# Four blocks of a modulation product moved from the full head pairs into the last head pair of an attention stage

## The reference

```
mod_l = split(silu(c)     @ ada_w[i] + ada_b[i], 6)     # for i = 0, 1
mod_c = split(silu(c_ctx) @ ada_w[i] + ada_b[i], 6)
q, k, v = h @ w_qkv + b_qkv                             # layer 0
o = softmax(q k^T * 64**-0.5 + bias) v                  # window keys + all context keys
x = x + gate * (o @ w_o + b_o)
```

## Time and profile before

| | |
|---|---|
| median of 3 executions | 2804.71 us |
| the profiled execution | 2803.35 us |
| its span (first to last instruction) | 2801.6 us |
| TensorE busy | 2571.0 us, 92% of the span |
| VectorE, ScalarE, GpSimd busy | 1082.8, 865.5, 478.1 us |
| line 687 (the ada blocks), TensorE | 384 matmul records, 49.6 us of record time |
| line 720 and 725 (pieces), TensorE | 296.2 and 151.6 us |
| line 570 (`rows`), VectorE | 20 instructions, 13.7 us |
| mean granted TensorE clock | 0.962 of full |

### The profile page before, as it was taken

How to read it: one execution, slowest core, us unless ns; L and a number is a source line. 1 busy time by engine, 2 the same in 40 slices (tenths; PEclk the granted TensorE clock), 3 DMA queues, 4 the chain that set the end, 5 groups by cost and what they waited for, 6 DMA issues and landing times. The chain is left out here.

```text
span 2801.6 us, 68712 instructions
## 1 busy us (share of the span) xinstructions
PE 2571.0 (92%) x28274; PEld 1803.8 (64%) x28275; DVE 1082.8 (39%) x2462; ACT 865.5 (31%) x1881; POOL 478.1 (17%) x590
## 2 busy tenths in 40 slices
PE   7999999999989849999999599999998699999990
PEld 6888788878745537777777484455444477777770
DVE  3134333433454532222222366556665322222225
ACT  3222322323210003333333355334500133333333
POOL 0111111121121012222222210000020122222223
PEclk9999999999999969999999799999999799999995
DMA  6322223132345287999999740000232999999995
GB/s 260 120 97 100 95 104 134 61 126 74 140 152 200 75 355 305 416 416 395 416 416 416 268 144 30 31 30 30 115 150 105 389 403 416 417 416 416 416 368 183
DMA packets 128670, 644.72 MB, mean 230 GB/s; under 512 B 18865, under 2 KB 31441, under 8 KB 72609
## 3 DMA queue, kind: packets, MB, share of 16 engines
q1 hardware_dynamic: 94912, 540.05, 48.5%
q0 software_dynamic: 17984, 57.16, 5.7%
q10 hardware_dynamic: 15648, 45.71, 4.2%
HBM read 578.29 MB, written 64.57 MB: 229 GB/s over the span
## 5 line engine op out<-in xcount | busy, mean ns | idle before, releaser
L1668 PE MATMUL PS<-wt,xT 128*32 128x256 f32 x13056 | 752.9, 381 | 38.3 <-DVE xT L1797 25.3
L1668 PEld LDWEIGHTS PS<-wt,xT 128*32 128x32 f32 x13056 | 513.0, 111 | 238.7 <-issue 47.9
L1613 ACT ACTIVATE y<-PS 32x256 f32<-32x256 f32 x816 | 306.3, 375 | 304.2 <-PE PS L1683 297.0
L1683 PE MATMUL PS<-wt,hidT 128*32 128x256 f32 x6528 | 395.2, 379 | 3.5 <-ACT y L1613 3.5
L1797 DVE STREAM_TRANSPOSE xT<-xg 128x256 f32<-128x256 f32 x206 | 91.8, 446 | 664.2 <-PE PS L1668 655.0
L1683 PEld LDWEIGHTS PS<-wt,hidT 128*32 128x32 f32 x6528 | 256.8, 110 | 99.3 <-issue 4.4
L720 PE MATMUL PS<-hT,slab 128*128 128x256 f32 x1280 | 296.2, 386 | 6.3 <-DVE low L613 3.5
L720 PEld LDWEIGHTS PS<-hT,slab 128*128 128x128 f32 x1280 | 239.9, 192 | 42.9 <-issue 6.5
L433 POOL TENSOR_SCALAR prob<-prob,inv 128x640 f32<-128x640 f32 (+2 forms) x80 | 130.3, 1629 | 662.2 <-DVE inv L628 662.2
L1573 POOL DMA_INDIRECT xg<-h_d,ib x212 | 208.3, 983 | 166.8 <-POOL ib L1570 166.0
L511 ACT ACTIVATE prob<-prob,low 128x640 f32<-128x640 f32 (+2 forms) x160 | 117.6, 735 | 300.2 <-DVE low L613 300.2
(11 more groups left out here) (247 smaller groups left out, 2653.4 us busy)
## 6 DMA issues: line engine op xcount, KB each, us to landing
wt<-in_w SPq DMA_DIRECT2D x256, 1024.0 KB, 11.9
wt<-in_w2s SPq DMA_DIRECT2D x128, 1024.0 KB
aw<-in_ada_w SPq DMA_DIRECT2D x48, 1024.0 KB, 4.9
ys_d<-y ACTq DMA_DIRECT2D x204, 128.0 KB
slab<-in_slabs SPq DMA_DIRECT2D x24, 512.0 KB, 3.3
tab<-in_tables SPq DMA_DIRECT2D x8, 1408.0 KB, 7.5
ys_d<-zero POOLq DMA_DIRECT2D x4, 2560.0 KB, 9.6
x_d<-x_p ACTq DMA_DIRECT2D x18, 512.0 KB, 4.8
```

What stands on the lines that cost most here:

```text
L1613: ins = a.activation(y[rows, q * QD:q * QD + QD], PS[STRIP * q:STRIP * q + STRIP, DOWN, 0:QD], ACT.Copy)
L1668: mm = t.matmul(PS[32 * g:32 * g + 32, UP, 0:QD], xT[:, k * 32:k * 32 + 32], wt[b][:, q, c * 1024 + g * QD:c * 1024 + g * QD + QD], start= ...
L1683: mm = t.matmul(PS[32 * g:32 * g + 32, DOWN, 0:QD], hT_[:, k * 32:k * 32 + 32], wt[b][:, q, c * 1024 + g * QD:c * 1024 + g * QD + QD], sta ...
```

## The change

The counts by pair change, and the last pair gets a list of how many blocks each of its ten units takes. Pairs 2, 3, 5 and 6 do one block fewer each, units 70, 71, 72 and 74 do two (the second one after values(i-1)), units 73, 75, 76 and 77 one. All 48 blocks are still done in the same order, and the last one still in unit 77.

```diff
-        BLOCKS = (5, 5, 5, 5, 4, 4, 4)
+        BLOCKS, LATE = (5, 5, 4, 4, 4, 3, 3), (2, 2, 2, 1, 2, 1, 1, 1, 0, 0)
...
             else:
-                if t < KD:
-                    first.append(("ada", KD + sum(BLOCKS) + t))
+                n = KD + sum(BLOCKS) + sum(LATE[:t])
+                if LATE[t]:
+                    first.append(("ada", n))
+                if LATE[t] > 1:
+                    second.append(("ada", n + 1))
             return first, second
```

## The result

The changed kernel takes 2809.18 us (median of 20 runs) beside 2804.61 us (20 runs of the kernel before): ratio 1.0017, 95% interval 1.0010 to 1.0024. The forecast was 3.6 us over before, measured are 4.6 us (2.8 to 6.7 by the interval). The median is within 0.2% and on the slow side. The interval does not reach down to 1, so the kernel is slower, if only by 0.10 to 0.24%.

What follows compares the result with a forecast made beforehand. Bound by TensorE in full pairs, by a loop of waits (scores, lows, exponential, copy, values) in the last. -3.9 + 3.9 + 3.2 + 0.4 + 0 = +3.6 us: 2808.3 us; own range 2806.5 to 2809.9, 8-in-10 range 2803.6 to 2812.4.

Steps and rivals of the forecast that it cites:

- Removed blocks: Full pairs 2, 3, 5 and 6: each block taken out shortens its unit on TensorE, -3.9 us in sum.
- Second blocks: Units 70, 71, 72 and 74: each block between values and scores adds 0.97 us to the loop, +3.9 us.
- The wait for rows(4): Unit 72: block 40 waits on TensorE for VectorE's rows(4) and holds up values(71), +3.2 us.
- Block 47: Unit 77: its load, now issued behind load_first, lands late beside the clearing; 0 to 1.0 us, taken as +0.4.
- The far bound: Block 47's load in unit 77: the clearing goes wholly first, so it lands at 803.6, a cost of 5.8 us.
- The clock: Last pair: one fall of 1.7 us, either behind the new stall or at the pair's end; net 0.
- Rival 2: Last pair: the clock falls both behind the stall and at the end, +5.3 us, 2810.0 us; chance 20%.

Runs made afterwards that it cites:

- e1: Changed kernel with the second blocks of units 70, 71, 72 and 74 moved before values: 2805.57 us, ratio 1.0004 to the kernel before.
- e3: Changed kernel with 15 extra matmuls, results unused, on TensorE ahead of block 40's wait: 2804.49 us, ratio 1.0000 to the kernel before.
- e6: e5 with load_first left in unit 74, ahead of block 46's load: 2810.35 us, ratio 1.0024 to the kernel before.
- e2: Kernel before with only one block moved out of the full pairs, unit 72 taking two: 2808.21 us, ratio 1.0013.
- e7: Kernel before with its last block in unit 78 in place of unit 77: 2799.30 us, ratio 0.9987.
- e9: e8 with six extra matmuls, results unused, in unit 72, which has no block: 2797.95 us, ratio 0.9979 to the kernel before.
- e4: Changed kernel with unit 72 left without a block and load_first issued in unit 76: 2805.73 us, ratio 1.0002 to the kernel before.
- e5: e4 with the five second blocks moved before values: 2799.12 us, ratio 0.9987 to the kernel before.
- e8: e5 with the last block in unit 78: 2796.90 us, ratio 0.9976 to the kernel before.
- e10: e8 run once more, unchanged, on the chip of e9: 2797.09 us, ratio 0.9977 to the kernel before.

## Why the prediction was right, step by step

- **Removed blocks, -3.9 us: right.** t = 8 and t = 6 units lost 0.97 us each.
- **Second blocks, +3.9 us: right.** Units 70, 71 and 74 are 0.97, 0.97 and 0.98 us longer; e1 takes it back by moving them ahead of values.
- **The wait for rows(4), +3.2 us: right**, to 0.1 us: rows(4) end 6.67 us after scores(72), as worked out, and block 40 starts at 6.72 for 6.77.
- **Block 47, +0.4 us: it cost nothing.** e3, where the clock stays at full as the forecast had it, tests this term. Counted from scores(72) the load landed after 36.6 us (the stated range is 34.3 to 38.0) and was wanted after 36.4, as worked out. The idle behind it covered the delay. In the change itself it landed 0.9 us before its use. The far bound, the clearing going wholly first, was not seen: in e6 both queues moved side by side, though block 46's load came 12.8 us late there.
- **The clock, 0 us: mis-sized.** The forecast took one fall out of two and so nothing on balance. Rival 2 came about instead: the clock fell behind the wait and again at the pair's end, where the thin stretch had moved along with the rest. The first fall lasted twice as long as the row of before that priced it (6.8 against 3.4 us) and cost 2.8 us, not 1.7. e3 shows it.

By the terms the last pair grew by 3.9 + 3.2 + 2.8 = 9.9 us, less 0.2 in unit 79; measured 9.7. With -3.9 this makes +5.8. The medians give +4.6, with an interval from 2.8 to 6.7 us. So the mechanism held but for the clock, and the closeness of 3.6 to 4.6 is in part luck: by the profile's terms the sum lies above the forecast's own range (1.8 to 5.2 us over before), nearer to rival 2's 5.3. The falls of the clock outside the change (prologue, 1.2 us in this profile) lie differently from execution to execution, and one profile cannot say how long the fall in unit 72 is on the mean: e2 had 3.4 us, e1 and the change 6.8.

The loss at the end of the pair, was taken as given. Its longest idle (1.71 us) was itself a wait behind rows(5), which e7 removed; the prediction read the idle and did not ask who ended it.

## What to carry to other kernels

Filler work is free on one side of a wait, as long as it fits into the idle (two blocks into 2.0 us here), and costs its full length on the other: read in the timeline in which gap of the bounding engine it falls. Where filler comes in groups that share a buffer, the handover between two groups must not fall into a stretch without other work; move the boundary before moving the quantity. Removing one wait or one fall of the clock in a loop of engines may only uncover the next (e9), so price a fix by what is late behind it.

## What was not expected of the hardware

- The granted clock fell behind a unit with 1.94 us of idle (e4, e5, e6, e8, e10), where the same loop with a block in every unit and 0.97 us of idle kept it at full. The levels were the full and the half (2.4 and 1.2 GHz). The length of one idle does not settle it: behind 1.71 or 1.72 us at the end of the pair the clock fell in seven profiles and not in e5, and behind 1.59 and 1.34 us in e7 it did not fall.
- One fall lasted 3.4 us in e2 and 6.8 us in e1 and in the changed kernel, behind idle stretches of nearly the same length (4.00, 4.12 and 4.12 us).
- Block 46's load in e6, 1 MB behind `load_first` and beside the clearing, landed 34.5 us after scores(73); the sum of the queue's rows had given 25.
